# Up projection of a feed-forward block by seven products of quarters instead of eight, with the lows of two of the seven weights made by GpSimd

## The chip, the cores and the metric

The kernel runs on one core of one Trainium2 chip. The metric is the device time of one execution in microseconds (us), the median of several runs. All matrix products are fp32 accuracy made of three fp32r matmuls: each operand is split into a high part (its rounded copy) and a low part (what is left), and high x high, low x high and high x low are added up in PSUM.

## The reference

One transformer layer over a prompt of 2048 tokens and 8 x 16 sampled tokens (2176 tokens, 17 tiles of 128). What the change touches is the feed-forward part of it and what hands the tokens over to it:

```python
D_MODEL = 1024; D_FF = 2816; CONV_W = 3
def conv_ffn(h, conv_hist, w_up, w_dw, b_dw, w_down):
    up = h @ w_up                                    # tokens x 1024 @ 1024 x 5632
    T = up.shape[1]
    ext = jnp.concatenate([conv_hist.astype(up.dtype), up], axis=1)
    c = ext[:, 0:T] * w_dw[0] + ext[:, 1:T + 1] * w_dw[1] + ext[:, 2:T + 2] * w_dw[2] + b_dw
    a, b = jnp.split(c, 2, axis=-1)
    return (jax.nn.silu(a) * b) @ w_down, ext[:, -(CONV_W - 1):]
...
    x1 = layer_norm(ALPHA * x + mix, ln1_g, ln1_b)
    ffn, new_conv = conv_ffn(x1, conv_hist, w_up, w_dw, b_dw, w_down)
    ple = jax.nn.sigmoid(x1 @ w_pg) * (pe @ w_pe)
    x2 = layer_norm(ALPHA * x1 + ffn + ple, ln2_g, ln2_b)
```

## The kernel before, in words

The phases run one after the other: projections, heads, attention, the mix part (`mix`, L1852) and the feed-forward part (`ffn`, L2295). The mix part goes through the 17 tiles: output projection, residual, norm, transpose of the normed tile (`turn`), store of the transposed tile x1_t, gate product and the first half of y. In its last steps it also splits the first weights and tokens of the feed-forward part (`ahead`).

The feed-forward part takes the tokens in three blocks of 6, 6 and 5 tiles (768, 768 and 640 columns). The tokens of a block stay in SBUF as eight pairs of high and low (x_hi, x_lo, one per 128 of the 1024 inputs). Over them runs a loop over 11 pairs of features; a feature f is one 128-wide tile of the a half and one of the b half of w_up (22 of them). TensorE (L2746) computes for each feature 2 halves x 2 chunks of columns x 8 inputs x 3 matmuls = 96 matmuls into four banks ps_u (`rows`), and for each pair of features the down products of the pair before (`downs`: 12 matmuls of 512 columns per tile, two banks of ps_d at a time). Order in the loop: rows of the even feature, downs, rows of the odd feature.

Behind each chunk ScalarE (L2565) copies the bank to `up` with two columns of history in front, and starts the convolution (`ff_cv_a`, `ff_cv_b`) with the middle tap and the bias straight from the bank. VectorE (L2640) adds the two other taps (`convolve`), multiplies silu(a) by b (`gate`) and adds the down products to y (`add`, L2682). ScalarE makes silu and the high of the product, GpSimd (L2457) its low and the lows of all weights, 1024 columns each, from three raw buffers; SP loads those. All engines run in program order with semaphores between them:

```python
act.wait_ge(upped, per_f(b, f, 4, 2 * s + c))
...
act.activation(cv[s][:, a:a + w], ps[:, 0:w], ACT.Identity, scale=taps[:, s, at_f, 2:3],
               bias=taps[:, s, at_f, 3:4]).then_inc(evac, 1)
```

A block ends with the second norm of its tiles, beside the opening of the next one.

## Time and profile before

| | |
|---|---|
| median of 3 runs | 3024.73 us (3021.55 to 3024.91) |
| the profiled execution, first to last instruction (span) | 3021.1 us |
| feed-forward part in it | 1442 us to the end |
| TensorE busy | 2938.2 us, 97% |
| VectorE, ScalarE, GpSimd busy | 54%, 45%, 46% |

The table is of one profiled execution beside the median of the unprofiled runs: the profile gives the span alone, and the median lies 3.6 us above it. A busy TensorE is not TensorE at its peak, since matmuls overlap; how far apart they start says what one costs. Idle time of an engine that nobody waits for costs nothing. In the profile PE is TensorE's matmuls, PEld its weight loads, DVE VectorE, ACT ScalarE, POOL GpSimd and SP the engine that issues the transfers.

### The profile page before, as it was taken

What the parts mean: (1) busy time and instruction counts of PE and PEld (TensorE: products, weight loads), DVE (VectorE), ACT (ScalarE), POOL (GpSimd) and SP (SyncE); (2) the same over time, 40 slices, a digit from 0 to 9 for tenths busy, and PEclk for the clock granted to TensorE, in tenths of its full rate; (3) what the DMA queues carried; (4) which work ended last, traced back from release to release, by engine and by line L of the source; (5) the groups of instructions that cost most, each with busy time, mean ns of one, the idle gap of its engine ahead of it and who ended that gap; (6) DMA issues with size and microseconds to landing.
All of it is one profiled execution on the core that took longest, in us unless ns stands there. A gap on an engine that the chain in (4) does not pass through costs nothing.

```text
span 3021.1 us, 43561 instructions
## 1 busy us (share of the span) xinstructions
PE 2938.2 (97%) x15389; PEld 2586.1 (86%) x15389; DVE 1618.7 (54%) x2178; ACT 1352.3 (45%) x2632; POOL 1393.3 (46%) x830
## 2 busy tenths in 40 slices
...
GB/s 137 87 66 144 137 174 58 43 55 52 47 43 130 120 89 89 89 89 96 175 53 72 56 69 56 96 155 70 56 69 56 69 70 150 102 72 67 80 72 61
DMA packets 161774, 262.10 MB, mean 87 GB/s; under 512 B 48352, under 2 KB 91072, under 8 KB 160288
## 3 DMA queue, kind: packets, MB, share of 16 engines
...
q8 instruction: 62, 1.02, 0.1%
q14 instruction: 48, 0.39, 0.0%
...
## 4 chain that ended last, share of the span: by engine, by line
PE 51%; DVE 1%; POOL 0%; issue 0%; DVEq 0%; ACTq 0%
PE ff_u L84 12%; PE ff_u L86 12%; PE ff_u L85 11%; PE ff_d L84 6%; PE ff_d L85 6%; PE ff_d L86 6%; DVE ff_y L2682 0%; DVE ff_y L2731 0%; DVE ff_stats L2714 0%; POOL ff_y L2517 0%; POOL ff_rstd L2507 0%; DVEq L2297 0%; DVE ff_mv L2716 0%; DVE ff_neg_mean L2718 0%; POOL ff_offset L2509 0%
## 5 line engine op out<-in xcount | busy, mean ns | idle before, releaser
L2467 POOL TENSOR_TENSOR ff_w_lo<-ho_raw,ff_w_hi 128x1024 fp32r<-128x1024 f32 x99 | 242.9, 2467 | 491.1 <-ACT ff_w_hi L2540 491.1
L2467 POOL TENSOR_TENSOR mx_w_lo<-ho_raw,mx_w_hi 128x1024 fp32r<-128x1024 f32 x97 | 276.0, 2859 | 230.9 <-ACT mx_w_hi L2540 230.9
L2661 DVE SCALAR_TENSOR_TENSOR ff_cv_a<-ff_up_a,ff_taps,ff_cv_a 128x768 f32<-128x768 f32 (+1 forms) x132 | 154.7, 1172 | 346.9 <-ACT ff_cv_a L2589 338.9
L2682 DVE TENSOR_TENSOR ff_y<-ff_y,ff_d 128x512 f32<-128x512 f32 x374 | 239.6, 681 | 146.3 <-PE ff_d L86 146.2
L2661 DVE SCALAR_TENSOR_TENSOR ff_cv_b<-ff_up_b,ff_taps,ff_cv_b 128x768 f32<-128x768 f32 (+1 forms) x132 | 122.7, 929 | 305.4 <-ACT ff_cv_b L2589 296.8
L1564 POOL TENSOR_TENSOR at_p_lo<-at_p,at_p_hi 128x512 fp32r<-128x512 f32 (+2 forms) x160 | 187.6, 1173 | 163.9 <-ACT at_p_hi L1601 162.2
L84 PE MATMUL ff_u<-ho_hi,mx_w_hi 128*128 128x384 f32 (+1 forms) x690 | 224.9, 326 | 0.7 <-ACTq L2533 0.7
L86 PE MATMUL ff_u<-ho_lo,mx_w_hi 128*128 128x384 f32 (+1 forms) x690 | 225.0, 326 | 0.0
L85 PE MATMUL ff_u<-ho_hi,mx_w_lo 128*128 128x384 f32 (+1 forms) x690 | 224.8, 326 | 0.0
L1594 ACT ACTIVATE at_p<-at_s 128x512 f32<-128x512 f32 (+1 forms) x320 | 170.2, 532 | 111.1 <-PE at_s L1790 56.0
L1706 DVE TENSOR_TENSOR at_p_lo<-at_p,at_p_hi 128x512 fp32r<-128x512 f32 (+1 forms) x160 | 187.3, 1171 | 45.5 <-ACT at_p_hi L1601 44.6
L84 PE MATMUL ff_u<-ho_hi,ff_w_hi 128*128 128x384 f32 x630 | 205.1, 326 | 0.0
L86 PE MATMUL ff_u<-ho_lo,ff_w_hi 128*128 128x384 f32 x630 | 205.0, 325 | 0.0
L85 PE MATMUL ff_u<-ho_hi,ff_w_lo 128*128 128x384 f32 x630 | 205.0, 325 | 0.0
L1601 ACT ACTIVATE at_p_hi<-at_p 128x512 fp32r<-128x512 f32 (+1 forms) x320 | 179.0, 560 | 0.0
L2580 ACT ACTIVATE ff_up_b<-ff_u 128x384 f32<-128x384 f32 x110 | 54.2, 493 | 268.8 <-PE ff_u L86 268.8
L84 PE MATMUL ff_d<-ff_w_hi,ff_h_hi 128*128 128x512 f32 x408 | 159.1, 390 | 4.4 <-DVE ff_y L2682 4.4
L2473 POOL TENSOR_TENSOR ff_h_lo<-ff_h,ff_h_hi 128x768 fp32r<-128x768 f32 (+1 forms) x66 | 118.2, 1791 | 91.3 <-ACT ff_h_hi L2600 91.3
L2674 DVE TENSOR_TENSOR ff_h<-ff_cv_a,ff_cv_b 128x768 f32<-128x768 f32 (+1 forms) x66 | 158.0, 2393 | 3.6 <-ACT ff_cv_a L2611 0.4
L85 PE MATMUL ff_d<-ff_w_hi,ff_h_lo 128*128 128x512 f32 x408 | 159.1, 390 | 0.0
L86 PE MATMUL ff_d<-ff_w_lo,ff_h_hi 128*128 128x512 f32 x408 | 159.1, 390 | 0.0
L2540 ACT ACTIVATE ff_w_hi<-ho_raw 128x1024 fp32r<-128x1024 f32 x99 | 103.3, 1049 | 123.2 <-DMA ho_raw<-in_w_ffn_p 123.2
...
## 6 DMA issues: line engine op xcount, KB each, us to landing
ho_raw<-in_w_ffn_p SPq DMA_DIRECT2D x196, 512.0 KB, 3.6
ho_raw<-in_x SPq DMA_DIRECT2D x17, 512.0 KB, 4.3
mx_m_raw<-scratch_mix_t SPq DMA_DIRECT2D x17, 512.0 KB, 5.2
scratch_x_t<-mx_work SPq DMA_DIRECT2D x17, 512.0 KB, 3.2
scratch_y<-mx_work SPq DMA_DIRECT2D x17, 512.0 KB, 3.0
ff_y<-scratch_y SPq DMA_DIRECT2D x17, 512.0 KB, 6.2
out_y<-ff_y SPq DMA_DIRECT2D x17, 512.0 KB, 2.7
ho_raw<-in_x_t SPq DMA_DIRECT2D x32, 256.0 KB, 3.1
```

The lines of the kernel that those rows point to most:

```text
L84: pe.matmul(out, lh, rh, start=first, stop=False, **kw)
L85: pe.matmul(out, ll, rh, start=False, stop=False, **kw)
L86: return pe.matmul(out, lh, rl, start=False, stop=last, **kw)
L1564: pool.tensor_tensor(p_lo[:, e % H_RING, 0:b - a], p[:, e % P_RING, 0:b - a], f32(p_hi[:, e % H_RING, 0:b - a]), ALU.subtract).then_inc(lo ...
L1594: act.activation(p[:, i % P_RING, 0:b - a], ps_s[i % S_BANKS][:, 0:b - a], ACT.Exp).then_inc(expd, 1)
L1601: act.activation(p_hi[:, i % H_RING, 0:b - a], p[:, i % P_RING, 0:b - a], ACT.Copy).then_inc(hid, 1)
L1706: dve.tensor_tensor(p_lo[:, e % H_RING, 0:b - a], p[:, e % P_RING, 0:b - a], f32(p_hi[:, e % H_RING, 0:b - a]), ALU.subtract).then_inc(lo_ ...
L2467: pool.tensor_tensor(w_lo[slot], w_raw[n % RAWS].rearrange("p (k c) -> p k c", c=P), f32(w_hi[slot]), ALU.subtract).then_inc(wlo, 1)
L2473: pool.tensor_tensor(h_lo[:, i + extra, 0:w], h[:, i, 0:w], f32(h_hi[:, i + extra, 0:w]), ALU.subtract)\
L2661: op = dve.scalar_tensor_tensor(cv[s][:, 0:pw], up[s][:, k:k + pw], tap, cv[s][:, 0:pw], ALU.mult, ALU.add)
L2674: dve.tensor_tensor(h[:, i, 0:w], cv[0][:, 0:w], cv[1][:, 0:w], ALU.mult).then_inc(mul, 1)
L2682: dve.tensor_tensor(y[:, t, H[i]], y[:, t, H[i]], ps_d[2 * (t % 2) + i][:, :], ALU.add)\
```

## The change

The up projection of a block is cut into quarters: the weights of a feature into A11, A12 (a half; first and second 512 inputs) and A21, A22 (b half), the tokens of a tile into left and right 64 columns and low and high 512 inputs. Seven products of a quarter with a quarter, in the order A11, A12, S2, S1, S3, S4, A22 (Winograd's form), replace eight. Each is 4 x 3 = 12 matmuls of 384 columns (320 in block 2), 84 a feature.

- **Sums of tokens** (T1 to T4) are made once, in the mix part: per tile four subtractions of 256 columns on GpSimd (`form`) in the buffer `gate`, stored in place of the plain tile, beside three plain quarters. The sigmoid writes `gate` only after that store has landed.
- **Sums of weights** (S1 to S4) are made in `combine`, four ops of 512 columns per feature on GpSimd, two features ahead of TensorE. All weight units are 512 columns now, with one raw buffer each (A22 two), and the down weights come in four pieces a pair through one buffer `d_raw`.
- **Banks**: A11, S2, S3, A22 accumulate on one bank (two banks, by turns). ScalarE copies it out behind each of the four (`copy`, L2800), and the next may start only then. A12 and S4 have the bank uz, S1 the bank uy; VectorE adds those (and uy twice) into `up` (`join`, L2967).
- **Convolution**: ScalarE starts it from `up` once the last join is in (`begin`, L2835). The gate is written over `cv_a`, its high and low are single, and VectorE makes the low.
- **Lows of weights**: VectorE makes five of seven; GpSimd those of S3 and S4, the fifth and sixth product.
- Down products now stand between S3 and S4 of the even feature, the last of a block behind A12 of the next block's first feature.

```diff
+POOL_W = (S3, S4)
+DVE_W = tuple(j for j in range(PRODUCTS) if j not in POOL_W)
...
+            def form(t):
...
+                pool.wait_ge(tcopy, at(t, 2, 1))
+                pool.wait_ge(st_y, (t + 1) * 16)
+                pool.tensor_tensor(t1, low_right, low_left, ALU.subtract).then_inc(formed, 1)
+                pool.tensor_tensor(t3, high_right, low_right, ALU.subtract).then_inc(formed, 1)
...
-                act.wait_ge(st_y, (t + 1) * 16)
+                act.wait_ge(st_x, (t + 2) * 48)
...
+            def load_down(b, p, at_d, m):
+                if m > 0:
+                    sp.wait_ge(dlo, down_n(b, p, m - 1))
...
+                sp.dma_start(d_raw[:, :], piece(at_d, m // 2, CW * (m % 2), CW)).then_inc(d_in, 16)
...
+            def combine(b, f, pf, par, ops=range(4)):
...
+                if 0 in ops:
+                    pool.wait_ge(combined, sum_n(pb, pf_, 3))
+                    pool.wait_ge(raw_in[A11], 16 * (b * FT + f + 1))
+                    pool.wait_ge(raw_in[S1], 16 * (b * FT + f + 1))
+                    weight_low(b, f, pb, pf_, S3)
+                    pool.wait_ge(*low_done(pb, pf_, S3))
+                    pool.tensor_tensor(s3, a11, s1, ALU.subtract).then_inc(combined, 1)
+                    pool.wait_ge(combined, sum_n(b, f, 0))
+                    pool.wait_ge(raw_in22[par], 16 * (b * PAIRS_F + pf + 1))
+                    pool.tensor_tensor(s1, s1, a22, ALU.add).then_inc(combined, 1)
+                    pool.wait_ge(combined, sum_n(b, f, 1))
+                    pool.tensor_tensor(s2, s1, a11, ALU.subtract).then_inc(combined, 1)
+                if 3 in ops:
+                    pool.wait_ge(combined, sum_n(b, f, 2))
+                    pool.wait_ge(raw_in[A12], 16 * (b * FT + f + 1))
+                    weight_low(b, f, pb, pf_, S4)
+                    pool.wait_ge(*low_done(pb, pf_, S4))
+                    pool.tensor_tensor(s4, a12, s2, ALU.subtract).then_inc(combined, 1)
...
+            def copy(b, f, par, k):
+
+                s, right, j = ((0, 0, A11), (0, 1, S2), (1, 1, S3), (1, 0, A22))[k]
+                pb, pf = following(b, f, -1)
+                act.wait_ge(conv, per_f(pb, pf, 4, 1 if s == 0 else 3))
+                act.wait_ge(prod, per_f(b, f, PRODUCTS, j))
...
+            def period(b, f, p, i, before, x_next=False, centring=None):
...
+                if before is not None:
+                    finish_up(*before)
+                carry_in(b, f, p, i, 0)
+                if before is not None:
+                    weights(b, f, (A22,), p, i)
+                    activate(*before[:4])
+                if i == 1:
+                    down_highs(b, p, (0, 1) if at_end(b, p) else (1,))
+                copy(b, f, i, 0)
+                if more:
+                    weights(nb, nf, (A11,))
+                carry_in(b, f, p, i, 1)
+                if before is not None:
+                    product_hi(*before[:4])
+                if more:
+                    weights(nb, nf, (A12,))
...
+                copy(b, f, i, 1)
+                if more:
+                    weights(nb, nf, (S2,))
...
+                if i == 1:
+                    down_highs(b, p, (2,))
+                if more:
+                    weights(nb, nf, (S1,))
...
+                copy(b, f, i, 2)
+                if more:
+                    weights(nb, nf, (S3,))
...
+                if not at_end(b, p) or i == 1:
+                    down_highs(b, p, (3,) if i == 1 else (0,))
+                if more:
+                    weights(nb, nf, (S4,))
...
+            tokens(0, (T2, T1))
+            act.wait_ge(const_in, 16)
...
+                    if j == A11:
+                        pe.wait_ge(copied, per_f(qb, qf, 4, 3))
+                    elif j == A12:
+                        pe.wait_ge(joined, per_f(pb, pf, 4, 3))
+                    elif j == S2:
+                        pe.wait_ge(copied, per_f(b, f, 4, 0))
+                    elif j == S1:
+                        pe.wait_ge(joined, per_f(pb, pf, 4, 2))
+                    elif j == S3:
+                        pe.wait_ge(copied, per_f(b, f, 4, 1))
+                    elif j == S4:
+                        pe.wait_ge(joined, per_f(b, f, 4, 0))
+                    else:
+                        pe.wait_ge(copied, per_f(b, f, 4, 2))
...
+                    multiply(b, 2 * q + 2, 0, before_downs)
+                    downs(b, q)
+                    multiply(b, 2 * q + 2, 0, after_downs)
+                    multiply(b, 2 * q + 3, 1, range(PRODUCTS))
```

ScalarE, one feature before (ff_u are the banks of the up projection, ff_up the copies with history, ff_carry the two columns carried from block to block):

```order
L2573 ACTIVATE ff_up_a<-ff_carry 128x2 [waits ff_carried,ff_conv]
L2580 ACTIVATE ff_up_a<-ff_u 128x384 [waits ff_upped]
L2589 ACTIVATE ff_cv_a<-ff_u,ff_taps 128x384 [waits ff_mul,ff_silu]
L2580 ACTIVATE ff_up_a<-ff_u 128x384 [waits ff_upped]
L2589 ACTIVATE ff_cv_a<-ff_u,ff_taps 128x384 [waits ff_mul,ff_silu]
L2595 ACTIVATE ff_carry<-ff_up_a 128x2 [waits ff_evac]
L2573 ACTIVATE ff_up_b<-ff_carry 128x2 [waits ff_carried,ff_conv]
```

The same engine after, around the turn from an even feature to an odd one (ho_hi is the high of A22, mx_odd that of a down piece, mx_w_hi that of A11 of the next feature):

```order
L2835 ACTIVATE ff_cv_a<-ff_up_a,ff_taps 128x768 [waits ff_hlo,ff_joined]
L2819 ACTIVATE ff_carry<-ff_up_a 128x2
L2800 ACTIVATE ff_up_b<-ff_u 128x6x64 [waits ff_prod,ff_conv]
L2835 ACTIVATE ff_cv_b<-ff_up_b,ff_taps 128x768 [waits ff_mul,ff_copied,ff_joined]
L2819 ACTIVATE ff_carry<-ff_up_b 128x2
L2809 ACTIVATE ff_up_a<-ff_carry 128x2 [waits ff_carried,ff_conv]
L2775 ACTIVATE ho_hi<-ff_w_raw 128x512 [waits ff_prod,ff_raw_in22_1]
L2852 ACTIVATE ff_cv_a<-ff_cv_a 128x768 [waits ff_conv]
L2784 ACTIVATE mx_odd<-ff_d_raw 128x512 [waits ff_down,ff_d_in]
L2800 ACTIVATE ff_up_a<-ff_u 128x6x64 [waits ff_prod,ff_conv]
```

The last row is the copy of the new feature's A11, which TensorE waits for; the begins, silu (L2852, which waits for the convolution) and two highs of the feature before stand ahead of it.

VectorE after, the first ops in a feature:

```order
L2979 SCALAR_TENSOR_TENSOR ff_cv_a<-ff_up_a,ff_taps,ff_cv_a 128x768 [waits ff_begun]
L2979 SCALAR_TENSOR_TENSOR ff_cv_a<-ff_up_a,ff_taps,ff_cv_a 128x768 [waits ff_conv]
L2979 SCALAR_TENSOR_TENSOR ff_cv_b<-ff_up_b,ff_taps,ff_cv_b 128x768 [waits ff_begun]
L2979 SCALAR_TENSOR_TENSOR ff_cv_b<-ff_up_b,ff_taps,ff_cv_b 128x768 [waits ff_conv]
L2990 TENSOR_TENSOR ff_cv_a<-ff_cv_a,ff_cv_b 128x768 [waits ff_conv,ff_silu]
L2949 TENSOR_TENSOR ho_lo<-ff_w_raw,ho_hi 128x512 [waits ff_whi]
L2949 TENSOR_TENSOR mx_w_lo<-ff_w_raw,mx_w_hi 128x512 [waits ff_whi]
L2967 TENSOR_TENSOR ff_up_a<-ff_up_a,ff_uz 128x6x64 [waits ff_copied,ff_prod]
L2995 TENSOR_TENSOR ff_h_lo<-ff_cv_a,ff_h_hi 128x768 [waits ff_hhi]
```

Convolution and gate of the feature before come first, then two weight lows, a join and the hidden low; before the change only convolution, gate and adds stood on this engine.

GpSimd after, for one feature and the four down pieces of a pair (L2658 the lows of S3 and S4, L2671 to L2682 the sums, L2688 the lows of down pieces):

```order
L2658 TENSOR_TENSOR mx_w_lo<-ff_w_raw,mx_w_hi 128x512 [waits ff_raw_in3,ff_whi,ff_raw_in0,ff_combined]
L2671 TENSOR_TENSOR ff_w_raw<-ff_w_raw 128x512 [waits ff_wlo_pool]
L2674 TENSOR_TENSOR ff_w_raw<-ff_w_raw 128x512 [waits ff_raw_in22_0,ff_combined]
L2676 TENSOR_TENSOR ff_w_raw<-ff_w_raw 128x512 [waits ff_combined]
L2688 TENSOR_TENSOR mx_odd<-ff_d_raw,mx_odd 128x512 [waits ff_dhi]
L2658 TENSOR_TENSOR mx_w_lo<-ff_w_raw,mx_w_hi 128x512 [waits ff_whi,ff_raw_in1,ff_combined]
L2682 TENSOR_TENSOR ff_w_raw<-ff_w_raw 128x512 [waits ff_wlo_pool]
L2688 TENSOR_TENSOR mx_odd<-ff_d_raw,mx_odd 128x512 [waits ff_dhi]
```

The first low of a feature waits for the raw S1 of two features on (ff_raw_in3) before it starts; for the other feature of a pair the same six ops stand without down pieces between them.

## Rows read from the trace of the kernel before

**Rows 1.** The page, busy us, share and count of each engine.
```profile
PE 2938.2 (97%) x15389; PEld 2586.1 (86%) x15389; DVE 1618.7 (54%) x2178; ACT 1352.3 (45%) x2632; POOL 1393.3 (46%) x830
```
**Rows 2.** Stretches of the feed-forward part: length, busy PE, PEld, DVE, ACT, POOL, clock, DMA.
```profile
1442.00:1988.00 546.00, 544.39 (x2895) 513.19 (x2896) 243.65 (x259) 217.60 (x390) 236.83 (x103) 1.00 0.24 84
1988.00:2536.00 548.00, 546.53 (x2906) 514.89 (x2905) 258.23 (x279) 217.25 (x389) 251.78 (x116) 1.00 0.23 80
2536.00:2986.00 450.00, 448.72 (x2723) 424.22 (x2721) 232.20 (x322) 201.09 (x506) 214.44 (x97) 1.00 0.24 84
```
**Rows 3.** Timeline of TensorE: start us, duration us, then engine, line, operation.
```profile
1850.05 0.39 PE L84 MATMUL ff_d<-mx_w_hi,ff_h_hi 128*128 128x512 f32 x1
...
1852.77 0.39 PE L84 MATMUL ff_d<-mx_w_hi,ff_h_hi 128*128 128x512 f32 x1
...
1860.35 0.33 PE L84 MATMUL ff_u<-ho_hi,mx_w_hi 128*128 128x384 f32 x1
...
1864.51 0.33 PE L84 MATMUL ff_u<-ho_hi,mx_w_hi 128*128 128x384 f32 x1
...
2703.32 0.28 PE L84 MATMUL ff_u<-ho_hi,ff_w_hi 128*128 128x256 f32 x1
...
2706.18 0.40 PE L84 MATMUL ff_d<-ff_w_hi,ff_h_hi 128*128 128x512 f32 x1
```
**Rows 4.** Timeline of VectorE in blocks 0 and 1.
```profile
1841.20 2.18 DVE L2661 SCALAR_TENSOR_TENSOR ff_cv_b<-ff_up_b,ff_taps,ff_cv_b 128x768 f32<-128x768 f32 x2 [5.32 <-ACT ff_cv_b L2589]
...
1874.23 1.02 DVE L2661 SCALAR_TENSOR_TENSOR ff_cv_b<-ff_up_b,ff_taps,ff_cv_b 128x768 f32<-128x768 f32 x1 [6.13 <-ACT ff_cv_b L2589]
...
1890.87 2.19 DVE L2661 SCALAR_TENSOR_TENSOR ff_cv_b<-ff_up_b,ff_taps,ff_cv_b 128x768 f32<-128x768 f32 x2 [5.31 <-ACT ff_cv_b L2589]
...
1935.32 4.18 DVE L2661 SCALAR_TENSOR_TENSOR ff_cv_a<-ff_up_a,ff_taps,ff_cv_a 128x768 f32<-128x768 f32 x2 [6.15 <-ACT ff_cv_a L2589]
```
**Rows 5.** Timeline of ScalarE, the copy behind a chunk of up matmuls.
```profile
1860.55 0.49 ACT L2580 ACTIVATE ff_up_a<-ff_u 128x384 f32<-128x384 f32 x1 [3.17 <-PE ff_u L86]
```
**Rows 6.** Instructions of a tile: count, shortest/median/longest ns, first and last start, shapes.
```profile
L2148 DVE TENSOR_TENSOR mx_t_lo<-mx_work,mx_t_hi x34: 684/693/695, 1020.7 to 1424.1; 128x512 fp32r<-128x512 f32 x34
L2682 DVE TENSOR_TENSOR ff_y<-ff_y,ff_d x374: 672/680/690, 1495.6 to 3004.6; 128x512 f32<-128x512 f32 x187
L365 POOL TENSOR_TENSOR pj_t_lo<-pj_sq,pj_t_hi x20: 455/1290/1312, 51.0 to 272.1; 128x512 fp32r<-128x512 f32 x16, 128x128 fp32r<-128x128 f32 x4
L2467 POOL TENSOR_TENSOR ff_w_lo<-ho_raw,ff_w_hi x99: 2386/2407/3130, 1450.8 to 2963.6; 128x1024 fp32r<-128x1024 f32 x99
L1601 ACT ACTIVATE at_p_hi<-at_p x320: 301/622/655, 482.8 to 979.5; 128x512 fp32r<-128x512 f32 x128, 128x256 fp32r<-128x256 f32 x32
L2611 ACT ACTIVATE ff_cv_a<-ff_cv_a x66: 723/832/847, 1463.4 to 2972.4; 128x768 f32<-128x768 f32 x44, 128x640 f32<-128x640 f32 x22
L2562 ACT ACTIVATE ff_y<-ff_y,ff_offset,ff_rstd x17: 1228/1244/1252, 1986.3 to 3009.0; 128x1024 f32<-128x1024 f32 x17
```
**Rows 7.** Timeline of GpSimd beside the last of rows 4.
```profile
1933.22 5.47 POOL L2467 TENSOR_TENSOR mx_w_lo<-ho_raw,mx_w_hi 128x1024 fp32r<-128x1024 f32 x2
```
**Rows 8.** Transfers: KB each, median us from issue to landing.
```profile
ho_raw<-in_w_ffn_p SPq DMA_DIRECT2D x196, 512.0 KB, 3.6
ho_raw<-in_x_t SPq DMA_DIRECT2D x32, 256.0 KB, 3.1
ho_raw<-scratch_q_t SPq DMA_DIRECT2D x8, 768.0 KB, 8.4
```
**Rows 9.** Stretches around two idle gaps of TensorE, columns as in rows 2.
```profile
508.50:510.70 2.20, 0.04 (x1) 0.00 (x0) 2.17 (x4) 1.11 (x2) 2.20 (x2) 1.00 0.00 0
510.70:514.00 3.30, 3.29 (x14) 2.75 (x15) 3.30 (x7) 1.31 (x3) 0.83 (x2) 0.71 0.00 0
1416.00:1418.40 2.40, 0.30 (x3) 0.03 (x1) 1.40 (x3) 1.08 (x2) 0.40 (x1) 1.00 0.00 0
1418.40:1422.30 3.90, 3.88 (x20) 3.07 (x20) 2.25 (x2) 0.34 (x1) 0.00 (x0) 1.00 0.50 159
```

1065 lines of the change are left out of this document (658 added, 407 removed).

## The prediction

> **What bounds the kernel now.** I read the busy shares first: TensorE is busy 97% of the span, the other three about half of it [rows 1]. The stretches of the feed-forward part come next: from 1442 us to the last down product TensorE is idle 1 to 2 us in 550 and its clock is at 2.4 GHz [rows 2]. So every matmul that leaves is worth its issue interval, as long as nobody makes TensorE wait. The intervals are read from start to start, since durations overlap: 24 up matmuls of 384 columns start 4.16 us apart (0.173 each), 24 of 256 columns 2.86 (0.119), 12 down matmuls of 512 columns 2.72 (0.227) [rows 3]. VectorE shows the period of a pair of features in blocks 0 and 1: the same op comes back after 49.67 us [rows 4]. Of that 2 x 96 x 0.173 = 33.3 are up and 6 x 2.71 = 16.2 down products. The engines behind have room: each bank is evacuated by ScalarE alone, 0.2 us after its chunk ends [rows 3, 5].
>
> **What the change takes away.** Per feature 96 up matmuls become 7 products of 12, with 384 columns still: 12 x 0.173 = 2.08 us less. Blocks 0 and 1 have 44 features: 91.5 us. In block 2 a feature took 48 x 0.173 + 48 x 0.119 = 14.0; now 84 of 320 columns, between the two intervals at 0.146, 12.3: 22 x 1.75 = 38.6 us. If TensorE stayed the bound, the whole gain would be 130 us. The moving operand is now read in six runs of 64 columns; no row here prices that. I take nothing for it and keep 0.01 us a matmul (5,500 of them, 55 us) for the upper end.
>
> **What it adds, and where.** Four sums of raw weights and two lows a feature, four lows of down pieces a pair, all 512 columns on GpSimd: 16 ops a pair at 1.29 [rows 6], 20.6 us. VectorE gets five lows (0.69), four joins from PSUM (384 columns, about 0.55 by the 0.68 of the adds), four convolution steps (1.02), gate and hidden low (0.95 by the same rate): 12 us a feature beside the adds. ScalarE: 9 highs a feature (0.62), four copies (0.49), two begins of 768 columns (1.03, from 1.24 at 1024), silu, hidden high (0.83): 12 us [rows 5, 6]. A feature without down products has 14.6 us of TensorE, so each queue fits by sum alone. The order decides, and two things in it:
> - The copy of the first product must be out before the third starts, one product (2.08 us) later. On ScalarE it stands behind silu of the feature before, and that behind two convolution steps on VectorE.
> - GpSimd and VectorE don't run beside each other when both read two SBUF tensors. The two steps of convolution from 1935.32 take 4.18 instead of 2.2 us; a GpSimd op lies between them, and two of those take 5.47 instead of 2 x 2.39 [rows 4, 6, 7]. They take turns; the one that waits hides 0.15 to 0.2 of its fixed part. With 512 columns a turn is 1.14 + 0.82 = 1.97 us.
>
> On the turns the Trainium skill (SBUF — State Buffer, "SBUF: two separate sides") says that the pair of ports is an exclusive lock for the whole instruction and the loser fully blocks. By that nothing is hidden and a turn is 2.31, not the 1.97 that the rows give.
>
> **One pair in blocks 0 and 1, walked from the end of its down products (t = 0).** PE-to-engine 0.2 [rows 3, 5], between other engines 0.05 to 0.15.
> 1. S4 ends 2.1, its join 2.8, the first begin 2.9 to 3.9, the copy of A22 4.9, the second begin 6.0. The convolution of the a half asks at 4.1, meets GpSimd's low of S4 (until 4.3) and sum S4, ends 7.1 (6.3 alone).
> 2. ScalarE: carry, high of A22, silu (to 8.7), high of down piece 1 (9.2), copy of A11 9.1 to 9.6. S2 of the odd feature starts at 9.7, not 8.3: **1.4 us**.
> 3. The down pieces have one raw buffer. High 1 at 9.2, low 10.6, load 3.1 (256 KB landed in 3.1, 512 KB in 3.6 [rows 8]) 13.8, high 2 14.5, low 16.3 behind a VectorE low, load 19.5, high 3 20.2. Behind it on ScalarE stand the high of S4 (20.8) and the first begin of the odd feature, 20.7 to 21.7, although its last join is done at 19.3.
> 4. GpSimd waits for the raw S1 of two features on; its buffer is freed by VectorE's low at 18.3, so it lands at 21.5. Six GpSimd ops then stand in a row just as the odd feature's convolution asks (21.9): first op until 23.0, a half 23.8 and 25.8, silu 27.4, copy of A11 27.8. The even feature started at 20.1, its A12 ended 24.3, S2 starts at 27.9: **3.6 us**.
> 5. Turns again: b half 29.7, gate 31.7, hidden high 32.6, high of A12 33.1, copy of S2 33.5. S3 starts at 33.6, S1 ended 32.1: **1.5 us**. S3 ends 35.7, the hidden low 35.6, so down products run from 35.8 to 52.0.
>
> The pair takes 52.0 instead of 49.7 us: TensorE's 45.4 and 6.6 of stalls. 22 pairs: +52 us.
>
> **Block 2.** The other engines' chain hardly shrinks: 640 columns instead of 768, but convolution, join, copy and begin are two instructions each. The same walk reaches the down products at about 36.4; these are 5 x 2.71 = 13.6, so 50.0, against 28.1 + 13.6 = 41.6 before. Ten pairs: +84 us.
>
> **The rest.** Opening: three token pieces of 768 KB and the taps are queued behind four weight loads, and ScalarE waits for the taps before its first copy; 12 us (the nearest piece of this size landed in 8.4 [rows 8]; ends 4 and 18). Two block turns, with token splits under the down products: 3 us each (0 to 8). In the mix part the four sums per tile (256 columns, about 0.75 each) and the longer stores fall beside gate products of 10.9 us (48 x 0.227): nothing, and if that cover is gone 1 us a tile, 17. The tail's chain is that of before: nothing.
>
> **Sum.** Own span 3021.1 + 52 + 84 + 12 + 6 = 3175; the median of the runs lies 3.6 above the span, so 3179. Roundings in ten steps of the walk lean up (register waits in the loop, 0.05 each, are left out: 33 pairs x 0.2): **3185 us**, 5% slower.
>
> **Rivals.**
> - **A, TensorE stays the bound** (faster). It decides by one point: silu is over before A12 ends, so the pair's stalls stay under 4.2 us in blocks 0 and 1 and 3.5 in block 2. With 0.5 us of stall a pair: 3024.7 - 130 + 12 + 6 + 17 = 2930. For it: sums of work fit on every engine [rows 6]. Against: steps 2 to 4. Chance 0.14.
> - **B, the chain without the turns.** If a convolution step pays only its own 1.02, step 1 ends 6.3, the stalls are 0.5 and 2.1, the pair 48.0; in block 2 43.9. Then 22 x -1.7 + 10 x 2.3 + 18 = +4: 3028, from 2990 to 3080. Against it: 4.18 us for two steps [rows 7]. Chance 0.15.
> - **C, forecast:** chain and turns, 3110 to 3235. Chance 0.50.
> - **D, the clock falls as well.** After a gap of 2.2 us at 508.5 the granted clock was 0.71 for the next 3.3 us, after one of 2.1 at 1416.3 it stayed at 1.00 [rows 9]: so TensorE goes to 1.2 GHz behind some stalls of this size and not behind others. Here a stall of 3.6 us a pair (8 in block 2) comes 33 times. S2 and S1 at half speed, of which step 5 hides 1.5 us, cost 0.6 to 2.5 us: +20 to +80, so 3205 to 3265. Chance 0.18. (With the skill's blocking in full, seven turns at 0.34 more are 2.4 us a pair and +79: 3264, inside this case.)
> - **E, the products themselves are slower** because of the 64-column runs: +55 on A, B or C. Chance 0.03.
>
> **How the numbers follow.** Likeliest is C, 3185. Its own range with D is 3110 to 3265. To leave out no more than 2 in 10 the range has to take in B and the slow half of E: 2985 to 3275. No change (within 0.2%, 6 us, about what a measurement of this kernel can tell) gets 0.03 out of B; faster is A and a third of B, 0.19; slower 0.78.
>
> **What would show it.** Right: up matmuls still 0.173 us apart, about 13% fewer (5,544 for 6,336); TensorE's idle time ahead of ff_u in hundreds of us, released by ScalarE's copies; a steady pair of 52 us in blocks 0 and 1 and of 50 in block 2; convolution ops with means well over 1.02. Wrong at step 4: a pair near 46 and VectorE ops at 1.0 (A), or near 48 (B). Wrong at step 3: the third down high ends before S4's join. Wrong on D: granted clock 1.00 in the feed-forward stretches. A slower mix part or an opening over 18 us would also break the sum.

## The result and the profile after

The changed kernel takes 3302.97 us, median of 4 runs (3301.61 to 3308.25), against 3023.14 us before (3019.70 to 3024.91, 4 runs): 1.093 times as long, 95% interval 1.0917 to 1.0950. The forecast was 3185 with a range to 3275. It had the sign and not the size: 280 us more, 162 forecast. The profiled execution spans 3299.8 us, 124.8 more than the 3175 of the sum.

The page of the changed kernel, as in [rows 1]:

```profile
PE 2918.6 (88%) x14597; PEld 2538.9 (77%) x14597; DVE 2183.9 (66%) x2932; ACT 1478.0 (45%) x2981; POOL 1621.2 (49%) x1153
```

TensorE issues 792 matmuls fewer than before, exactly what seven products for eight take away, and is busy for almost as long (2918.6 for 2938.2 us). Behind some stalls it works at the lower clock: the granted clock is 0.94 over this span and was 0.98 over that of the kernel before. What it waits for, the waits of TensorE in us in total, times, longest:

```profile
PE ff_u L84 <- ACT ff_up_a L2800: 235.2, 67, 11.5
PE ff_d L84 <- issue: 23.2, 2, 11.9
PE ff_d L84 <- DVE ho_raw L3003: 18.5, 4, 9.7
PE ff_u L84 <- ACT ff_up_b L2800: 13.8, 6, 7.4
```

The first row is in the main the wait that the forecast was made of. Single waits of 7 to 12 us are not in its walk; one of them, for the taps in the opening, is in the forecast's term for the opening. Stretches of the feed-forward part, columns as in [rows 2]: the opening, block 0, the turn to block 1, block 1, the turn to block 2, block 2 and its end. The cuts are the starts of down products, but for the last, at 3260:

```profile
1441.00:1522.00 81.00, 48.38 (x228) 46.90 (x227) 43.54 (x38) 32.80 (x56) 43.05 (x23) 0.77 0.46 145
1522.00:1994.00 472.00, 429.93 (x2163) 397.96 (x2162) 336.76 (x379) 194.53 (x378) 223.42 (x144) 0.96 0.19 60
1994.00:2198.00 204.00, 151.98 (x720) 137.87 (x719) 152.07 (x167) 80.84 (x139) 115.34 (x69) 0.87 0.30 104
2198.00:2617.50 419.50, 380.70 (x1923) 352.15 (x1922) 300.53 (x339) 172.68 (x336) 199.08 (x128) 0.97 0.19 61
2617.50:2815.00 197.50, 139.67 (x711) 126.43 (x710) 152.21 (x199) 81.81 (x184) 107.00 (x69) 0.84 0.30 102
2815.00:3174.00 359.00, 296.78 (x1598) 276.56 (x1597) 249.67 (x392) 159.88 (x435) 155.59 (x112) 0.90 0.19 61
3174.00:3260.00 86.00, 70.99 (x383) 65.71 (x382) 55.89 (x95) 37.96 (x105) 30.41 (x22) 0.90 0.17 44
3260.00:3299.80 39.80, 17.11 (x75) 13.54 (x73) 25.25 (x44) 6.22 (x5) 17.25 (x15) 0.79 0.17 66
```

Nine pairs in 472 us are 52.4 each, eight in 419.5 also 52.4, seven of block 2 in 359 are 51.3. The walk gave 52.0 and 50.0. A turn, from the second last down products of a block to the second ones of the next, holds three pairs: 157 us at the steady rate (157.7 for the second, with its two down products of six tiles), and takes 204 and 197.5. So the steady pairs hold and the turns and the opening don't.

**One steady pair, beside the walk.** VectorE, then GpSimd, around the copy of the even feature's A11; the down products ended at 1800.4, which is the walk's t = 0:

```profile
1822.28 3.79 DVE L2979 SCALAR_TENSOR_TENSOR ff_cv_a<-ff_up_a,ff_taps,ff_cv_a 128x768 f32<-128x768 f32 x2 [2.89 <-ACT ff_cv_a L2835]
1826.00 3.98 DVE L2979 SCALAR_TENSOR_TENSOR ff_cv_b<-ff_up_b,ff_taps,ff_cv_b 128x768 f32<-128x768 f32 x2
1830.01 1.91 DVE L2990 TENSOR_TENSOR ff_cv_a<-ff_cv_a,ff_cv_b 128x768 f32<-128x768 f32 x1
1831.85 1.76 DVE L2949 TENSOR_TENSOR ho_lo<-ff_w_raw,ho_hi 128x512 fp32r<-128x512 f32 x1
```

```profile
1820.76 1.29 POOL L2688 TENSOR_TENSOR ho_lo<-ff_d_raw,ho_hi 128x512 fp32r<-128x512 f32 x1 [3.84 <-ACT ho_hi L2784]
1822.01 1.29 POOL L2658 TENSOR_TENSOR mx_w_lo<-ff_w_raw,mx_w_hi 128x512 fp32r<-128x512 f32 x1
1823.38 1.88 POOL L2671 TENSOR_TENSOR ff_w_raw<-ff_w_raw 128x512 f32<-128x512 f32 x1
1825.43 1.77 POOL L2674 TENSOR_TENSOR ff_w_raw<-ff_w_raw 128x512 f32<-128x512 f32 x1 [0.17 <-POOL ff_w_raw L2671]
1827.28 1.88 POOL L2676 TENSOR_TENSOR ff_w_raw<-ff_w_raw 128x512 f32<-128x512 f32 x1
1829.32 1.79 POOL L2658 TENSOR_TENSOR mx_w_lo<-ff_w_raw,mx_w_hi 128x512 fp32r<-128x512 f32 x1 [0.16 <-POOL ff_w_raw L2676]
1831.19 1.88 POOL L2682 TENSOR_TENSOR ff_w_raw<-ff_w_raw 128x512 f32<-128x512 f32 x1
```

The six ops of step 4, from the second row of GpSimd on, stand exactly against convolution and gate. They start behind the low of the fourth down piece (first row), which ends at 1822.05. The raw S1 for which step 4 lets them wait had landed at 1820.94, so that wait was over 1.1 us before; it is so in all 24 steady pairs. From 1823.38 to 1831.19 four turns take 7.81 us, 1.95 each. The forecast took 1.97 from [rows 7]. By the full blocking that the Trainium skill (SBUF — State Buffer, "SBUF: two separate sides") states a turn of these ops would have been 2.31; the trace does not show that. The walk has the copy of A11 at 27.3 to 27.8, and the trace has it at 1827.71, 27.3 after the down products.

**One pair of block 2.** TensorE behind its wait in the even feature (first matmuls of S2, S1 and S3), then ScalarE's copy of S2, for which S3 waits:

```profile
2910.18 0.63 PE L84 MATMUL ff_u<-mx_odd,mx_w_hi 128*128 128x320 f32 x1 [6.21 <-ACT ff_up_a L2800]
...
2913.54 0.47 PE L84 MATMUL ff_uy<-mx_odd,mx_w_hi 128*128 128x320 f32 x1
...
2915.88 0.31 PE L84 MATMUL ff_u<-ff_x_own,mx_w_hi 128*128 128x320 f32 x1
```

```profile
2914.07 0.48 ACT L2800 ACTIVATE ff_up_a<-ff_u 128x256 f32<-128x256 f32 x2
```

S2 and S1 take 5.7 us from the start of S2 to that of S3, where two products at 2.4 GHz take 3.5 in this block; the granted clock is 0.50 from 2910.1 to 2914.7, so 1.2 GHz. The copy is out at 2914.55, and TensorE comes to S3 only 1.3 us later. It does not wait again before the down products at 2917.64, for which the hidden low was out at 2915.18. In all seven steady pairs of block 2 S3 starts 1.2 to 1.5 us behind that copy. Here TensorE at the lower clock is what the pair waits for.

**One turn.** TensorE's waits of over 9 us between 1994 and 2198 us; the first is ahead of the last down products of block 0, the second ahead of S2 of the second feature of block 1, the third inside the first down products of block 1:

```profile
2049.88 0.77 PE L84 MATMUL ff_d<-mx_odd,ff_h_hi 128*128 128x512 f32 x1 [11.91 <-issue]
...
2096.49 0.66 PE L84 MATMUL ff_u<-mx_odd,mx_w_hi 128*128 128x384 f32 x1 [11.01 <-ACT ff_up_a L2800]
...
2149.29 0.79 PE L84 MATMUL ff_d<-mx_odd,ff_h_hi 128*128 128x512 f32 x1 [9.67 <-DVE ho_raw L3003]
```

What each waited for, on VectorE, ScalarE and VectorE again:

```profile
2048.22 1.55 DVE L2995 TENSOR_TENSOR ff_h_lo<-ff_cv_a,ff_h_hi 128x768 fp32r<-128x768 f32 x1
...
2147.95 2.48 DVE L3003 TENSOR_TENSOR ho_raw<-ho_raw,ff_d 128x512 f32<-128x512 f32 x4 [10.68 <-DMA ff_y<-scratch_y]
```

```profile
2095.33 0.63 ACT L2784 ACTIVATE mx_odd<-ff_d_raw 128x512 fp32r<-128x512 f32 x1 [8.05 <-DMA ff_d_raw<-in_w_ffn_p]
```

The first wait ends as the hidden low of the last feature is out (2049.77). The second ends with a copy that stands on ScalarE behind the high of the second down piece; that piece was requested at 2092.8, when GpSimd had made the low of the first, and GpSimd's low stood behind two scalings of the norm, a low and three sums. The third ends when VectorE gets the y of the new block, loaded behind the stores of the old one.

**The opening**, ScalarE: the first copy waits for the taps, the next two rows are highs of down pieces with a copy behind each:

```profile
1454.80 0.20 ACT L2809 ACTIVATE ff_up_a<-ff_carry 128x2 f32<-128x2 f32 x1 [11.05 <-DMA ff_taps<-in_taps]
...
1483.36 0.63 ACT L2784 ACTIVATE mx_odd<-ff_d_raw 128x512 fp32r<-128x512 f32 x1 [8.31 <-DMA ff_d_raw<-in_w_ffn_p]
...
1500.45 0.63 ACT L2784 ACTIVATE ff_d_own<-ff_d_raw 128x512 fp32r<-128x512 f32 x1 [10.89 <-DMA ff_d_raw<-in_w_ffn_p]
```

TensorE waits 10.4, 11.5 and 7.4 us for these three. The forecast knew the first.

### The profile page after: what moved, and what is told of

The parts are those of the page before. It is cut to its first block and busy times, and to the rows that moved or that the text cites. A ratio compares the mean times of both kernels' runs of the same rounds, so it can differ in the third digit from the quotient of the medians.

```text
span 3299.8 us, 47459 instructions
## 1 busy us (share of the span) xinstructions
PE 2918.6 (88%) x14597; PEld 2538.9 (77%) x14597; DVE 2183.9 (66%) x2932; ACT 1478.0 (45%) x2981; POOL 1621.2 (49%) x1153
## 5 line engine op out<-in xcount | busy, mean ns | idle before, releaser
L2658 POOL TENSOR_TENSOR mx_w_lo<-ff_w_raw,mx_w_hi 128x512 fp32r<-128x512 f32 x130 | 187.6, 1443 | 324.8 <-DMA ff_w_raw<-in_w_ffn_p 291.4
L84 PE MATMUL ff_u<-mx_odd,mx_w_hi 128*128 128x384 f32 (+1 forms) x264 | 117.3, 444 | 231.7 <-ACT ff_up_a L2800 231.7
L2979 DVE SCALAR_TENSOR_TENSOR ff_cv_a<-ff_up_a,ff_taps,ff_cv_a 128x768 f32<-128x768 f32 (+1 forms) x132 | 202.5, 1534 | 139.9 <-ACT ff_cv_a L2835 87.5
L3003 DVE TENSOR_TENSOR ho_raw<-ho_raw,ff_d 128x512 f32<-128x512 f32 x264 | 169.4, 684 | 187.6 <-PE ff_d L86 167.3
L2775 ACT ACTIVATE mx_w_hi<-ff_w_raw 128x512 fp32r<-128x512 f32 x390 | 242.1, 623 | 59.5 <-PE ff_uz L86 40.8
L2688 POOL TENSOR_TENSOR mx_odd<-ff_d_raw,mx_odd 128x512 fp32r<-128x512 f32 x66 | 106.9, 1620 | 292.5 <-ACT mx_odd L2784 292.5
L2949 DVE TENSOR_TENSOR mx_w_lo<-ff_w_raw,mx_w_hi 128x512 fp32r<-128x512 f32 x260 | 205.9, 810 | 38.8 <-ACT mx_w_hi L2775 38.1
L84 PE MATMUL ff_d<-mx_odd,ff_h_hi 128*128 128x512 f32 x364 | 144.8, 398 | 41.8 <-issue 23.2
L1679 DVE TENSOR_REDUCE at_neg_max<-mx_m 128x1 f32<-128x512 f32 (+2 forms) x214 | 128.4, 604 | 49.0 <-PE mx_m L1755 27.1
L86 PE MATMUL ff_d<-mx_odd,ff_h_hi 128*128 128x512 f32 x364 | 144.0, 395 | 0.0
L85 PE MATMUL ff_d<-mx_odd,ff_h_lo 128*128 128x512 f32 x364 | 143.9, 395 | 0.0
L1810 PE MATMUL at_o<-at_p_hi,at_v_one 128*66 128x512 f32 (+1 forms) x320 | 119.5, 373 | 3.4 <-DVE at_p_lo L1708 2.2
L3003 DVE TENSOR_TENSOR ff_y<-ff_y,ff_d 128x512 f32<-128x512 f32 x110 | 70.6, 684 | 71.8 <-PE ff_d L86 71.8
```

The costliest lines, as they stand in the source:

```text
L84: pe.matmul(out, lh, rh, start=first, stop=False, **kw)
L85: pe.matmul(out, ll, rh, start=False, stop=False, **kw)
L86: return pe.matmul(out, lh, rl, start=False, stop=last, **kw)
L2658: pool.tensor_tensor(w[j][1], w_raw[:, j, :], f32(w[j][0]), ALU.subtract).then_inc(wlo_pool, 1)
L2775: act.activation(w[j][0], raw, ACT.Copy).then_inc(whi, 1)
L2949: dve.tensor_tensor(w[j][1], raw, f32(w[j][0]), ALU.subtract).then_inc(wlo_dve, 1)
```

## The experiments

All are edits of the changed kernel. One table first, in us: the time (a single run, but for the last row, the median of 4), the opening (first product of the feed-forward part to its first down products), the mean pair of blocks 0 and 1, the two turns as defined above, and the pair of block 2. The kernel before was 3022 to 3026 beside them.

| kernel | time | opening | pair 0, 1 | turns | pair 2 |
|---|---|---|---|---|---|
| the change | 3303.0 | 81.4 | 52.4 | 204.3, 197.3 | 51.3 |
| e1 sums short | 3201.3 | 74.9 | 50.1 | 193.3, 182.5 | 47.7 |
| e2 two raw buffers | 3257.2 | 65.8 | 51.6 | 199.8, 196.5 | 50.7 |
| e3 copy first | 3301.1 | 80.4 | 52.7 | 203.7, 197.3 | 51.3 |
| e4 opening order | 3295.9 | 60.9 | 52.6 | 208.2, 203.1 | 51.3 |
| e5 lows on VectorE | 3298.3 | 78.4 | 52.9 | 199.2, 193.4 | 51.1 |
| e6 norm short | 3268.1 | 79.9 | 52.4 | 190.4, 185.7 | 51.3 |
| e7 last downs late | 3323.4 | 81.0 | 52.5 | 211.2, 207.6 | 51.3 |
| e8 GpSimd short | 3075.1 | 71.1 | 46.8 | 178.3, 166.1 | 43.8 |
| e9 y not loaded | 3278.2 | 80.3 | 52.2 | 191.6, 189.1 | 51.3 |
| e10 low before raw | 3308.9 | 79.5 | 52.7 | 203.6, 199.4 | 51.3 |
| e11 e8 + e6 + e9 | 3026.4 | 72.4 | 46.8 | 155.8, 148.1 | 43.4 |
| e12 clock filled | 3298.2 | 80.7 | 52.2 | 203.0, 198.9 | 51.1 |
| e13 e2 + opening | 3251.2 | 60.2 | 51.6 | 200.1, 195.5 | 50.7 |
| e14 down lows short | 3237.5 | 79.4 | 50.3 | 196.1, 190.4 | 49.8 |
| e15 e5 + e3 + opening | 3279.8 | 61.5 | 52.9 | 198.4, 193.9 | 51.2 |
| e16 e11 + opening | 3013.8 | 56.1 | 46.8 | 157.8, 147.3 | 43.7 |
| e17 down lows on VectorE | 3289.2 | 61.3 | 53.0 | 202.5, 199.4 | 51.3 |

**e1.** The sums of `combine` are made over `[:, 0:4]`.

> The four sums of raw weights a feature are made over 4 of 512 columns (from the second feature on), so the products S1 to S4 use stale weights; every instruction, wait and transfer stays. Port turns (theory T): eight of GpSimd's sixteen long ops a pair are gone and convolution finds GpSimd nearly idle, so a pair of blocks 0 and 1 takes about 48.5 us instead of 52.2 and one of block 2 about 45 instead of 51.2; with 22 and 10 pairs that is -140, and the openings of the blocks lose a few us more: 3130 to 3165. Order of the queues (theory Q): TensorE waits because down highs stand ahead of the first copy on ScalarE and come late through one raw buffer; sums hardly matter, the pair stays over 51 and the time over 3260.

Measured 3201: the pair falls by 2.3 and 3.6 us, neither T's 3.7 and 6.2 nor Q's 1. GpSimd's sums count, and are not all.

**e2.** Down pieces by turns through two buffers.

```diff
-                if m > 0:
-                    sp.wait_ge(dlo, down_n(b, p, m - 1))
+                if m > 1:
+                    sp.wait_ge(dlo, down_n(b, p, m - 2))
```

> Down pieces get two raw buffers instead of one, each with its own semaphore; to make room the shift of the second norm reads the gain in place of the offset, and the offset is not loaded. Theory Q: the third high is out at about 15 us after the down products instead of 20, the first begin of the odd feature starts at 19.4 instead of 20.7, so the pair loses 1.0 to 1.3 us in blocks 0 and 1 and as much in block 2 (-35), and the waits of 11 us ahead of TensorE's third product in each block's second feature go (-30): 3225 to 3245. Theory T: the six GpSimd ops meet the convolution wherever it begins, the pair stays at 52 and only the openings move: over 3265.

Measured 3257: the pair loses only 0.8 and 0.6, the opening 15.6, the turns 4.5 and 0.8. One raw buffer is a term of the opening, little in the pair.

**e3.** `copy(b, f, i, 0)` ahead of `down_highs`.

> ScalarE copies the first product of an odd feature before the high of the second down piece, not behind it. Theory Q for the blocks' openings: the waits of 11.5, 11.0 and about 11 us ahead of the third product of the second feature (released by that copy) go, the later ones stay or grow by part of it: -20 to -33 us; in the loop the copy is out 0.5 earlier but the high is 0.4 later, so the pair stays within 0.3 of 52.2: 3262 to 3285. Rival: the openings are bound by the down weights themselves, which then come as late for the down products; nothing gained, 3295 to 3305.

Measured 3301, the rival. In the opening the wait of 11.5 became 2.6, and 6.4 and 9.3 came behind it where 7.4 had been. A copy in front of a late high moves the wait to the next product; the pieces are no earlier.

**e4.** Taps first; `odd_loads(b, 1, ...)` ahead of the loads of y in block 0; GpSimd's `down_lows` ahead of sums and scalings.

> Openings only: the taps are the first transfer of the feed-forward part; in block 0 y, the norm's constants and the history are loaded behind the down pieces of the second feature; GpSimd makes the lows of a block's first down pieces ahead of that feature's sums and of all scaling of the norm. Theory Q: the wait of 10.4 at the first copy goes (-8 to -10), in block 0 the 11.5 and the 7.4 shrink to 5 together (-12), in the two later openings down pieces come 8 to 10 us earlier each, part of it lost again to later stores and loads of y (-10 in all): 3262 to 3275, steady pairs unchanged at 52.2 and 51.2. Rival: these transfers are as late in any order, because sums and scalings fill GpSimd: 3285 or more.

Measured 3296: the opening gained 20.5 us, as expected from the first two edits. The turns lost 3.9 and 5.8, where 10 of gain were expected; the rest is a start 1.4 us later and small differences of the pairs. In the first turn the wait for y is 10.7 where it was 9.7, and waits of 10.9 and 8.8 stand where 11.0 and 5.8 stood: with GpSimd's lows early its scalings are late.

**e5.** `POOL_W = ()`: the second part of the change undone.

> The second part of the change is undone: VectorE makes all seven weight lows, GpSimd the sums and the lows of down pieces. GpSimd's row of six ops at the turn to an odd feature becomes four, VectorE has 2.8 us more a pair. If GpSimd's port turns set the pair (T): the short-sums run took 2.0 us off a pair with half of GpSimd's long ops gone, so a quarter gone is about 1 us: pair 51.2, time 3265 to 3285. If VectorE's own queue sets it (V): its lows stand ahead of the joins and the pair grows to over 53: 3315 or more.

Measured 3298, between both: pair +0.5, turns -5.1 and -3.9. Where these two lows are made hardly matters; that part of the change is not what costs.

**e6.** Scaling, centring and shift over four columns.

> Scaling, centring and shift of the second norm act on 4 of 1024 columns; every instruction, wait and transfer stays. The two block turns took 204 and 197 us from the second last down products of a block to the second of the next, where three steady pairs take 157 and 155. If the sum of work on GpSimd and VectorE, taking turns at SBUF, sets the turn (T): six scalings of 2.4 to 3.1 and six shifts of 1.2 to 3 us go, the turn falls by 18 to 25 and the time by 36 to 50: 3250 to 3265. If the order sets it (down pieces' chain, last down products behind two products alone, y loaded behind stores, Q): under 6 us a turn, 3288 or more.

Measured 3268: -13.9 and -11.6 a turn, so nearer to Q than T's 18 to 25, and more than Q's 6: the norm's work is 30% of a turn's excess.

**e7.** Last down products behind S3; tokens T2 and B22 are split, and y is added, at other places of VectorE's queue accordingly.

> The last down products of a block stand behind the fifth product of the next block's first feature, as in the loop, not behind its second. Theory Q: TensorE's wait of 11.9 us ahead of them (the hidden low of the last feature is that late) is covered by three more products: -6 to -10 a turn, so 3280 to 3288. Rival: GpSimd's row of work behind them (statistics, scalings) only starts later and gives it back in the next feature: 3295 to 3305.

Measured 3323, worse than either (its feed-forward part began 4 us later as well). The wait moved to S2, which now stands ahead of the down products and needs the low of T2. VectorE made that behind the hidden low and beside GpSimd's token low, in 4.98 us where it takes 1.76 alone, until 2059.1:

```profile
2059.18 0.69 PE L84 MATMUL ff_u<-mx_odd,mx_w_hi 128*128 128x384 f32 x1 [17.41 <-DVE mx_odd L2956]
```

**e8.** Sums and lows by GpSimd over four columns; tokens and norm whole.

> All of GpSimd's steady work on 4 of 512 columns (sums, lows of the fifth and sixth weight and of down pieces; tokens and norm stay whole), so its results are stale; waits and transfers stay. If turns are what lifts the pair over TensorE's bound (T), this is rival B of the prediction or better: pair 48.0 or less, block 2 43.9 or less, and with the turns of blocks 10 us shorter each about 3300 - 95 - 73 - 20 = 3110, down to 3080. If ScalarE's order alone keeps the pair up (Q): pair over 49.5, block 2 over 46.5, time over 3150.

Measured 3075. The pair is 46.8, 5.6 less than in the change and 1.4 over TensorE's own 45.4; block 2's is 43.8, 0.1 from rival B's. That is what T said. But the run shortens GpSimd's links in the chain of the down pieces as well as the turns. Over 17 steady pairs each (means), the odd feature's convolution begins 19.5 us after the down products instead of 21.8, and from there to the end of the gate it is 5.3 us instead of 9.6: 2.3 us from an earlier start and 4.4 from turns in the odd feature, and 1.0 is given back behind the gate. Convolution by VectorE in steady pairs, busy us and mean ns, of the change and then of this run:

```profile
L2979 DVE SCALAR_TENSOR_TENSOR ff_cv_a<-ff_up_a,ff_taps,ff_cv_a 128x768 f32<-128x768 f32 x32 | 52.2, 1632 | 36.5 <-ACT ff_cv_a L2835 34.3
...
L2979 DVE SCALAR_TENSOR_TENSOR ff_cv_b<-ff_up_b,ff_taps,ff_cv_b 128x768 f32<-128x768 f32 x32 | 46.9, 1466 | 2.3 <-DVE ff_cv_b L2979 1.2
```

```profile
L2981 DVE SCALAR_TENSOR_TENSOR ff_cv_a<-ff_up_a,ff_taps,ff_cv_a 128x768 f32<-128x768 f32 x32 | 32.6, 1019 | 24.9 <-ACT ff_cv_a L2837 22.7
L2981 DVE SCALAR_TENSOR_TENSOR ff_cv_b<-ff_up_b,ff_taps,ff_cv_b 128x768 f32<-128x768 f32 x32 | 32.5, 1016 | 2.3 <-DVE ff_cv_b L2981 1.2
```

Every step takes 1.02, as in [rows 4], once GpSimd leaves SBUF alone.

**e9.** No `load_y` in blocks 1 and 2.

> In the second and third block y is not loaded anew (the sums go on from the block before, whose tiles are still stored), and the first add waits for the stores instead of the loads. Theory: TensorE's wait of 9.7 us inside the first down products of these blocks is six loads of 512 KB queued behind six stores; with them gone it falls to 0 to 3, the turn by 7 to 9, the time by 14 to 18: 3282 to 3287. Rival: the adds wait for the stores anyway (GpSimd's scalings and VectorE's shifts end late), wait 5 or more: 3292 to 3300.

Measured 3278: -12.7 and -8.2, and the wait of 9.7 is gone. The time came out 4 us under the expectation.

**e10.** `weight_low(..., S3)` ahead of the waits for the raw A11 and S1.

> GpSimd makes the low of S3 before it waits for the raw A11 and S1 of the feature after next, not behind that wait. Step 4 of the prediction (six ops in a row meet the convolution of the odd feature): five are left, the last contended op of VectorE (gate) runs alone, so a pair loses 0.9 us in blocks 0 and 1 and in block 2: about 3272 (3265 to 3280). Rival: the row still covers both convolutions, or the row starts later by the same amount; pair within 0.3, 3293 to 3303.

Measured 3309, within 6 us of the change (3 of them lie ahead of the feed-forward part). But the edit took no op out of the row. The low of the fourth down piece stands in front of it on GpSimd and ends after the raw S1 has landed (at 1825.46 here), so the same six ops follow it, as in the change, in every steady pair:

```profile
1825.38 1.30 POOL L2688 TENSOR_TENSOR ho_lo<-ff_d_raw,ho_hi 128x512 fp32r<-128x512 f32 x1 [4.01 <-ACT ho_hi L2784]
1826.63 1.29 POOL L2658 TENSOR_TENSOR mx_w_lo<-ff_w_raw,mx_w_hi 128x512 fp32r<-128x512 f32 x1
```

What five ops in place of six would give was not tested. The run shows that the wait which the edit goes around was not the one that counted.

**e11.** The edits of e8, e6 and e9 together.

> The short GpSimd ops of the eighth run, the short norm of the sixth and the y of the ninth together; only tokens are still split whole. If the excess of a block turn (38 and 30 us over three pairs of that run) is norm work (14 and 12) and y (9 each), it is now 15 and 9, and the time 3075 - 26 - 18 = 3031. If these only cover one another (a chain behind them of down pieces and last down products, theory Q), the excess stays over 22 and the time over 3045.

Measured 3026, excess 15.4 and 11.7: the terms nearly add up, as in the first reading.

**e12.** In front of S2 of even features:

```diff
+                            for n in range(FILL):
+                                pe.matmul(filler, w[j][0][:, 0:P], x0[:, :, 0, :], start=n == 0, stop=n == FILL - 1,
```

> Ahead of the third product of each even feature TensorE runs 16 matmuls into the idle bank, 2.8 us of the wait of 3.6 (6 in block 2); nothing reads them. Case D of the prediction priced the half clock behind this wait at 0.6 to 2.5 us a pair. If it costs that: the granted clock behind the wait is 1.00, the pair 51.0 to 51.6 and the time 3260 to 3285. Rival: the other engines' chain hides the slow products (the pair walked at full clock came to 52.0, measured 52.4), pair 52.0 to 52.5 and 3292 to 3302.

Measured 3298, pair 52.2: the rival. Windows of the change, the wait of 3.2 us and the two products behind it, and then of this run; the clock is the third number from the end:

```profile
1824.30:1828.20 3.90, 0.74 (x5) 0.42 (x3) 3.75 (x3) 1.92 (x5) 3.66 (x3) 1.00 0.00 1
1828.20:1832.20 4.00, 3.97 (x15) 3.96 (x16) 3.96 (x3) 0.86 (x3) 3.76 (x3) 0.65 0.00 0
```

```profile
1822.80:1827.90 5.10, 4.62 (x27) 4.29 (x25) 4.81 (x3) 2.75 (x7) 4.78 (x4) 1.00 0.14 51
1827.90:1832.00 4.10, 4.05 (x23) 4.05 (x24) 4.07 (x3) 0.91 (x3) 3.86 (x3) 1.00 0.00 0
```

The clock is back at 2.4 GHz and the pair is 0.2 us shorter: S2 and S1 were faster and TensorE then waited 1.2 us for the copy of S2. That holds for blocks 0 and 1. In block 2 the 16 matmuls end 3.7 to 4.9 us before S2, the granted clock is 0.92 over its pairs (0.90 in the change), and the run does not test the clock there as a whole. Its single pairs differ: where S2 took 2.2 to 2.4 us the pair took 50.6 to 50.9, where it took 3.4 us the pair took 51.5 to 51.6.

**e13.** e2, the taps first and y late in block 0, with GpSimd's order left alone.

> Two raw buffers for down pieces (as in the second run, with its shift of the norm by the gain), the taps as first transfer, and in block 0 the loads of y, constants and history behind the down pieces. If the wait for the taps (10.3 us in the second run) and the chain of down pieces are separate terms they add up: opening 67 - 9 = 58 or less, steady pairs 51.5 as in the second run, 3257 - 8 to - 14: 3243 to 3249. Rival: with taps in time the opening waits for the split tokens of GpSimd and VectorE instead, 3253 or more.

Measured 3251. The opening is 60.2, not 58: with the taps in time TensorE waits 7.3 us ahead of S3, for a copy that stands on ScalarE behind three token pieces as they land. Both readings are partly right.

**e14.** Only the lows of down pieces over four columns.

> Only the lows of down pieces on 4 of 512 columns. Between the run with short sums (pair 50.1) and the one with all GpSimd work short (46.7) lie the lows of down pieces and those of the fifth and sixth weight. If step 3 of the prediction (one raw buffer, a low of GpSimd in every link) has its weight here: the third down high comes 3 to 4 us earlier, begin 1.3 us earlier, pair 50.5 to 51.2, time 3245 to 3270. Rival: the row of six ops against the convolution hides it, pair within 0.4 of 52.4: 3285 or more.

Measured 3238, beyond the expectation: 2.2 us a pair, 1.5 in block 2, 8.2 and 6.9 a turn. The traces tell where the 2.2 lie (means of 17 steady pairs each): the odd feature's convolution begins 20.4 us after the down products instead of 21.8, and convolution and gate take 9.2 us instead of 9.6. So 1.4 us are shorter links, as expected, 0.4 fewer turns, and 0.3 lie behind the gate.

**e15.** All of the change's work, with e5, e3, taps first and y late in block 0.

> A kernel that computes all: seven lows on VectorE, copy of the first product before the high of the second down piece, taps first and y late in block 0. By the single runs (-4, 0, and 19 of opening where turns are not touched) 3275 to 3284. Rival: the late y is paid in the first adds, 3290 or more.

Measured 3280, as the sum of single runs said.

**e16.** e11 with taps first and y late in block 0.

> The eleventh run (short GpSimd ops, short norm, y not loaded) with taps first and y late in block 0. By the wait of 10.4 at the first copy and some of those of 6.4 and 5.9 behind it: 3026 - 10 to - 18, 3008 to 3016, below the kernel before for the first time: what seven products give if GpSimd costs nothing. Rival: the opening waits for tokens instead, over 3020.

Measured 3013.8 against 3026.5 of the kernel before: 0.4% under it, in one run, and only with most of GpSimd's work, the norm's scaling and the loads of y left out.

**e17.** As e15, with GpSimd keeping its two lows of weights and VectorE making those of down pieces:

```diff
+            def down_low(b, p, m):
+                dve.wait_ge(dhi, down_n(b, p, m))
+                hi, lo = down_piece(b, p, m)
+                dve.tensor_tensor(lo, d_raw[:, :], f32(hi), ALU.subtract).then_inc(dlo, 1)
```

> A kernel that computes all: VectorE makes the lows of down pieces (0.69 alone, where GpSimd took 1.3 to 2.0), each behind the work that comes at that time, GpSimd those of the fifth and sixth weight and the sums; the opening as in the fifteenth run. With the down lows short the pair was 50.2 (49.8 in block 2); four lows on VectorE are 2.8 us of it, three of them in the odd feature beside joins. If the links of the raw buffer's chain matter more than VectorE's load: pair 50.5 to 51.5, 3303 - 20 of opening - 30 to - 60: 3223 to 3253. Rival: VectorE's lows wait at the head of its queue for ScalarE's high and the joins behind them are late: pair over 52.4, over 3280.

Measured 3289.2 (3286.8 to 3292.1), ratio to the kernel before 1.0877 (1.0859 to 1.0895): the rival. VectorE, the low of the last piece and the join behind it, with the down products ended 20.3 us before the first row:

```profile
1805.69 0.69 DVE L2995 TENSOR_TENSOR ho_lo<-ff_d_raw,ho_hi 128x512 fp32r<-128x512 f32 x1 [3.22 <-ACT ho_hi L2784]
1806.30 0.55 DVE L2967 TENSOR_TENSOR ff_up_a<-ff_up_a,ff_uz 128x384 f32<-128x384 f32 x1
1808.37 3.30 DVE L2979 SCALAR_TENSOR_TENSOR ff_cv_a<-ff_up_a,ff_taps,ff_cv_a 128x768 f32<-128x768 f32 x2 [1.52 <-ACT ff_cv_a L2835]
```

VectorE stood 3.2 us at the head of its queue for that low, the last join began 21.0 us after the down products and was out at 21.5 where the walk had it at 19.3, and convolution still met GpSimd's sums. What e14 gained by leaving the lows out is not to be had by moving them there.

## Why the prediction was right and wrong

- **Steps 1 to 5 of the walk: right but for one cause.** 52.4 measured for 52.0, with the copies where the walk has them. E1 and e8 confirm what it rests on: with GpSimd's steady work short 5.6 us of the pair are gone, of 7.0 between 52.4 and TensorE's 45.4. Sums are 2.3 of it (e1), lows of down pieces 2.2 (e14). If the terms add up, which no run tested, the lows of two weights are the other 1.1, though on VectorE these cost no less (e5). The cause that was wrong is in step 4: GpSimd's row waits for the low of the fourth down piece, which the walk left out, and not for the raw S1. The two were over within about 1 us of each other, so the time of the row came out right by luck.
- **Step 3: right in the main.** The raw buffer's chain was given the delay of the odd feature's begin. Two buffers gave back 0.8 us (e2), not 1.3; shorter links with one buffer moved the begin by 1.4 us (e14).
- **Block 2: 51.3 for 50.0.** Short by 1.3 a pair, 13 us over ten. The trace puts these on the clock: S3 starts 1.2 to 1.5 us after its copy of S2 is out, because S2 and S1 run at the lower clock. The term for the other engines' chain was then right. Pairs of e12 with a fast and a slow S2 are 0.6 to 1.0 us apart, which points the same way; no run kept the clock up through block 2, so the cause is read from the trace and not shown by an experiment.
- **Turn prices: right.** 1.95 us a turn of 512 and 768 columns, 1.97 taken.
- **"Two block turns, with token splits under the down products: 3 us each (0 to 8)": this step failed.** They cost 47 and 40 us more than three steady pairs, 81 of the 118 us missed. The row of before that misled was right for its kernel: [rows 2] has TensorE idle for 1.5 us in the whole stretch from 1988 to 2536, which holds parts of both turns. The sentence took the cover for granted and did not walk the turn. For the first one, where the runs put its 47 us: norm on GpSimd, ScalarE and VectorE and y loaded behind stores 22.5 together (e11 against e8; alone 14, e6, and 13, e9), GpSimd's sums and lows 9 beyond what they cost in steady pairs (e8: 37.9 over its own 140.4), and 15.4 left (e11): the last down products behind two products only (a wait of 6.4 there), token splits on four engines' queues, and a slower clock. How the 15.4 divide was not settled; e7, which meant to take the first out, made it worse.
- **"Opening 12 (4 to 18)": too low.** 39.6 of TensorE, 12, and the stalls of a pair would be 58; measured 81.4. The wait for the taps was there (10.4). Not in the term were the waits of 11.5 and 7.4 behind the down pieces: step 3's chain, once with loads of 512 KB for y ahead of it in SP's queue. Taps first and y late took 20 us off (e4, e15), two raw buffers 16 (e2); the two overlap and took 21 together (e13).
- **Case D, the clock: happened, and cost little in blocks 0 and 1.** In the pair shown there the granted clock was 0.65 behind the wait, and e12 took that away for a gain of 0.2 us a pair, because the other engines set the period. Case D had 0.6 to 2.5. S2 and S1 took 5.9 us there where two products take 4.2, and 1.2 of these 1.7 us were a wait ahead of S3 in any case. In block 2 the clock cost about 1.3 us a pair by the trace, inside case D's price. What it cost in the turns was not settled.
- **Case E: excluded.** In e8's trace the twelve matmuls of a product, in runs of 64 columns, start from 1880.50 to the next product's 1882.58: 2.08 us, or 0.173 each as in [rows 3].
- **The mix part: right**, the first product after it starts 1.4 us earlier than before.

81 of turns, 23 of opening and 13 of block 2 are 117 of 118 us; what blocks 0 and 1 had over 52.0 (9 us) was about the allowance for roundings (6.6).

Rival A, 2930 us with TensorE as the bound, stayed far off: e16, with hardly anything on GpSimd, gives 3014.
